# ScalarE takes the norm factor before it rounds weights; first weight loads go out before the conditioning rows; conditioning columns move to other blocks

## The reference

```python
h = rms_norm(x, norm1_g);  proj = h @ w_in            # first layer
x = x + concat([ym, ya]) @ w_out                      # its output product
h2 = rms_norm(x, norm2_g)
x = x + peer(h2, w_query, keys, expert_u, expert_v)   # picked experts
# layers two (neighbourhood attention) and three (sliding window), each:
mod = silu(c) @ w_mod + b_mod                         # six vectors: shift, scale, gate, twice
h = modulate(rmsnorm(x, g_attn), shift, scale);  x = x + gate * (attention(h) @ w_o)
h = modulate(rmsnorm(x, g_ffn), shift2, scale2); x = x + gate2 * ffn(h)

def rms_norm(x, g):
    return x * lax.rsqrt(jnp.mean(x * x, axis=-1, keepdims=True) + EPS) * g
```

## Time and profile before

| | us |
|---|---|
| median of 3 runs | 4173.3 |
| lowest and highest run | 4167.85, 4173.65 |
| the profiled execution, its time | 4169.04 |
| its span | 4167.3 |
| PE busy in it | 3733.9 (90%) |
| DVE busy | 2649.3 (64%) |
| ACT busy | 1393.1 (33%) |
| POOL busy | 1412.3 (34%) |
| mean granted clock of TensorE | 0.938 |

### The profile page before, as it was taken

One profiled execution on the slowest core, in us unless ns is written; L12 is line 12 of the kernel. 1 busy time (PEld: TensorE's weight loads), 2 busy tenths in 40 slices (PEclk: granted clock), 3 DMA queues, 4 the chain that ended last, 5 costly groups with the idle time before them and its releaser, 6 DMA issues. The chain is left out here.

```text
span 4167.3 us, 56565 instructions
## 1 busy us (share of the span) xinstructions
PE 3733.9 (90%) x19126; PEld 3021.2 (72%) x19126; DVE 2649.3 (64%) x5251; ACT 1393.1 (33%) x1937; POOL 1412.3 (34%) x608
## 2 busy tenths in 40 slices
PE   8757789999999989999988989889998977788989
PEld 6634567778888778888877756568887866566867
DVE  7554778888777689999978546574544022744440
ACT  3205223334555322232222137622223122453331
POOL 3002433433333344444443125432222320243433
PEclk9857899999999999999998989989999988899999
DMA  5102344444554666666644340131111110012222
GB/s 208 50 26 89 131 144 139 147 140 143 191 183 159 223 204 189 197 190 197 190 139 155 111 79 1 62 106 66 60 60 49 62 41 33 6 41 91 96 77 89
DMA packets 242904, 475.43 MB, mean 114 GB/s; under 512 B 47307, under 2 KB 127179, under 8 KB 237804
## 3 DMA queue, kind: packets, MB, share of 16 engines
q1 hardware_dynamic: 222300, 433.11, 31.7%
q10 hardware_dynamic: 20480, 40.80, 2.6%
HBM read 397.82 MB, written 71.83 MB: 113 GB/s over the span
## 5 line engine op out<-in xcount | busy, mean ns | idle before, releaser
L329 POOL TENSOR_TENSOR w_low<-w_raw,w_high 128x1024 fp32r<-128x1024 f32 (+1 forms) x204 | 543.6, 2666 | 1079.2 <-ACT w_high L283 1079.2
L227 PE MATMUL psum<-h_high,w_high 128*128 128x512 f32 (+1 forms) x1696 | 627.1, 370 | 113.5 <-DVE h_low L566 78.8
L228 PE MATMUL psum<-h_low,w_high 128*128 128x512 f32 (+1 forms) x1696 | 619.8, 365 | 0.0
L229 PE MATMUL psum<-h_high,w_low 128*128 128x512 f32 (+1 forms) x1696 | 615.1, 363 | 0.0
L283 ACT ACTIVATE w_high<-w_raw 128x1024 fp32r<-128x1024 f32 (+1 forms) x204 | 226.6, 1111 | 905.9 <-PE psum L229 847.4
L1501 POOL TENSOR_TENSOR pick_u_low<-pick_u_raw,pick_u_high 128x1024 fp32r<-128x1024 f32 x128 | 312.3, 2440 | 568.0 <-ACT pick_u_high L1555 568.0
L227 PEld LDWEIGHTS psum<-h_high,w_high 128*128 128x128 f32 x1696 | 323.8, 191 | 191.9 <-issue 102.2
L1755 POOL TENSOR_TENSOR v_low<-v_raw,v_high 128x1024 fp32r<-128x1024 f32 x128 | 307.8, 2406 | 409.8 <-ACT v_high L1742 409.8
L227 PE MATMUL psum<-a_high,v_high 128*128 128x512 f32 x1024 | 399.7, 390 | 13.9 <-DVE v_context L1807 13.9
L227 PE MATMUL psum<-h_high,pick_u_high 128*128 128x512 f32 x1024 | 411.7, 402 | 0.0
L228 PE MATMUL psum<-h_low,pick_u_high 128*128 128x512 f32 x1024 | 403.9, 394 | 0.0
(11 more groups left out here) (378 smaller groups left out, 7090.2 us busy)
## 6 DMA issues: line engine op xcount, KB each, us to landing
pick_u_raw<-in_expert_uT SPq DMA_DIRECT2D x128, 512.0 KB, 3.5
v_raw<-in_expert_v SPq DMA_DIRECT2D x128, 512.0 KB, 3.8
mod_w<-in_w_mod SPq DMA_DIRECT2D x88, 512.0 KB, 3.6
w_raw<-in_ffn_up SPq DMA_DIRECT2D x88, 512.0 KB, 3.4
gelu_dram<-pick_gelu ACTq DMA_DIRECT2D x128, 256.0 KB, 2.0
gates_dram<-gate_plane SPq DMA_DIRECT2D x32, 1024.0 KB, 7.1
g<-gates_dram SPq DMA_DIRECT2D x64, 512.0 KB, 5.1
p<-gelu_dram SPq DMA_DIRECT2D x128, 256.0 KB, 5.0
```

What stands on the lines that cost most here:

```text
L227: nc.tensor.matmul(bank, w_high, x_high, start=first, stop=False)
L228: nc.tensor.matmul(bank, w_high, x_low, start=False, stop=False)
L229: return nc.tensor.matmul(bank, w_low, x_high, start=False, stop=last)
L329: nc.gpsimd.tensor_tensor(w_low[r % 2][:, :, :], raw[r % n_raw][:, :, :], w_high[r % 2][:, :, :].bitcast(F32), ALU.subtract).then_inc(k.w_ ...
```

## The change

Five things are done. (1) `Norm.scalar` is cut in two, and the new `Norm.factor` (Ln and Exp) stands on ScalarE ahead of the rounding of weights 0 and 1. (2) The table load that holds Ln and Exp is issued by ScalarE at the end of the block before, behind its last square; only the first block has it at its own start. (3) In `product`, SP issues the four weight loads of the first pass in a row, and the `mod_w` loads of that pass behind them; in later passes they alternate as before. (4) The columns move: `w_out` has no `side` any more; `w_query` takes columns 16 to 31 in place of 24 to 39; `na_o` takes 32 to 39 with two conditions in place of the second layer's last sixteen with one; `swa_q` takes these sixteen, two to a chunk. (5) In the expert values, `Squares` gets seven square buffers in place of two, GpSimd adds chunks 1 to 4 alone, and TensorE takes the last three squares directly.

```diff
 class Squares:
-    def __init__(self, k, pieces):
+    def __init__(self, k, pieces, at=PICKS_AT, buffers=None, direct=1):
...
     def total(self, pe):
-        pe.wait_ge(self.added.sem, self.added.at(KD - 2))
+        pe.wait_ge(self.added.sem, self.added.at(KD - 1 - self.direct))
         for i, (t0, n) in enumerate(self.pieces):
             self.nc.tensor.matmul(self.k.psum[:, i, 0:n], self.k.const("ones"), self.acc[:, t0:t0 + n], start=True, stop=False)
-        pe.wait_ge(self.squared.sem, self.squared.at(KD))
-        for i, (t0, n) in enumerate(self.pieces):
-            mm = self.nc.tensor.matmul(self.k.psum[:, i, 0:n], self.k.const("ones"), self.slot(KD - 1)[:, t0:t0 + n], start=False, stop=True)
+        for c in range(KD - self.direct, KD):
+            pe.wait_ge(self.squared.sem, self.squared.at(c + 1))
+            for i, (t0, n) in enumerate(self.pieces):
+                mm = self.nc.tensor.matmul(self.k.psum[:, i, 0:n], self.k.const("ones"), self.slot(c)[:, t0:t0 + n], start=False, stop=(c == KD - 1))
...
-        with sp.Fori(0, passes) as it:
+        def load(it, r):
+            sp.wait_ge(k.w_low.sem, k.w_low.at(it * RING + (r + 1)))
+            source = w[it * per + r // parts].rearrange("p (k n) -> p k n", n=P)[:, r % parts * kp:(r % parts + 1) * kp, :]
+            sp.dma_start(raw[r % n_raw][:, :, :], source).then_inc(k.weights_in[r % n_raw].sem, 16)
+
+        for r in range(RING):
+            load(0, r)
+        if side:
             for r in range(RING):
...
+                side.load(sp, 0, r)
+        if passes > 1:
+            with sp.Fori(0, passes - 1) as before:
+                it = before + 1
+                for r in range(RING):
+                    load(it, r)
+                    if side:
+                        side.load(sp, it, r)
...
         if norm:
             norm.squares(act)
+            norm.factor(act)
             round_weights(0, 0)
             round_weights(0, 1)
...
+            nc.scalar.preload_act_table_set("natural_log_exp_and_others")
             return
...
-        product(k, block, t["w_out"], KD, KD, LATENT, high, low, BIG + 2 * KD * SEQ, add_to_x(k, lambda c, i: 1.0, LATENT), full=f.mixT, sums=Squares(k, LATENT),
-                side=Modulation(k, t, ((2 * KD, 1, 2),), 40000, 34816))
+        product(k, block, t["w_out"], KD, KD, LATENT, high, low, BIG + 2 * KD * SEQ, add_to_x(k, lambda c, i: 1.0, LATENT), full=f.mixT, sums=Squares(k, LATENT))
...
-    sums = Squares(k, LATENT)
+    sums = Squares(k, LATENT, at + KD * CTX, KD - 1, 3)
...
-                side=Modulation(k, t, ((3 * KD, 1, 2),), 24832, 26880))
+                side=Modulation(k, t, ((2 * KD, 1, 2),), 24832, 26880))
...
-                side=Modulation(k, t, ((MODS + 4 * KD, 2, 1), (MODS + 4 * KD + 1, 2, 1)), BIG + 2 * KD * TOK, BIG + 2 * KD * TOK + 2 * D, 43008))
+                side=Modulation(k, t, ((4 * KD, 1, 2),), BIG + 2 * KD * TOK, BIG + 2 * KD * TOK + 2 * D, 43008))
...
-                norm=modulated_norm(k, layer, "g_attn", 0, both))
+                norm=modulated_norm(k, layer, "g_attn", 0, both),
+                side=Modulation(k, t, ((MODS + 4 * KD, 2, 1), (MODS + 4 * KD + 1, 2, 1)), BIG + 2 * KD * TOK, BIG + 2 * KD * TOK + 2 * D, 43008))
```

26 lines of the change are left out of this document (12 added, 14 removed).

## The result

| | before | changed |
|---|---|---|
| median, us (6 runs each, same series) | 4172.3 | 4148.3 |
| lowest and highest, us | 4167.85, 4173.65 | 4146.89, 4149.38 |
| time of the profiled execution, us | 4169.04 | 4147.98 |
| its span, us | 4167.3 | 4146.2 |
| mean granted clock | 0.938 | 0.939 |

The account below looks back on a forecast made before the run. The prediction took PE's waits as the bound, chiefly the chain ahead of the first `h_low`. It summed 11.3 + 9.0 - 8.5 - 1.3 + 2.2 = 12.7 us, giving 4160.6 us against the median 4173.3, range 4151 to 4169.

Parts of the forecast that it names:

- The factor first: Six norm blocks: Ln and Exp ahead of both weight roundings let newton and the first matmul start sooner, +11.3 us together.
- the six walks: Norm blocks walked singly: `w_query` 3.5, `na_qk` 6.1, first `ffn_up` 1.4, `swa_q` 1.7, last `ffn_up` 2.4, first block -3.8 us.
- Columns out of `w_out`: `w_out` without columns: 6.8 us from first matmul to `norm_v` and 2.2 us at its start, +9.0 us.
- Columns into `swa_q`: `swa_q` with two columns a chunk: weight loads stand behind row loads waiting for VectorE, -8.5 us, bounds -5 and -12.
- The wait at chunk 4: `swa_q`: weights for chunk 4 come late behind row loads, so that chunk starts 4.9 us late.
- The wait at chunk 7: `swa_q`: chunk 7 is delayed by another 0.9 us.
- the tail of 2 to 3 us: End of `swa_q`: VectorE's last columns end 2 to 3 us after PE.
- SP's new order costs nothing: SP's loads: no change of time, since row loads are needed only after the norm.
- The head norm's table load: Layer three: Silu leaves another table, so the head norm loads one between Ln and Exp, -1.3 us.
- The expert values: End of the expert values: the accumulator is ready sooner and PE does four warm sums, +2.2 us; nothing if cold.
- The splits slip in cheaper: Rival: GpSimd doesn't get between VectorE's back-to-back instructions, up to 2.3 us more in six blocks, near 4147; 8%.
- three slower rivals: `swa_q` dearer and norms less, 4168, 22%; SP's queue serial in `swa_q`, 4190, 4%; weights replace factor wait, 4170.6, 6%.

Follow-up runs that it names:

- factor_only: The kernel before with parts 1 and 2 alone (factor ahead of the roundings, table load in the block before): 4157.3 us, ratio 0.9964 to the kernel before.
- first_block_old_order: The changed kernel with the first block's two roundings ahead of its factor again: 4148.6 us, ratio 0.9947 to the kernel before.
- columns_back: The changed kernel without part 4, the columns back where they were before: 4155.3 us, ratio 0.9962 to the kernel before.
- sums_old: The changed kernel without part 5, GpSimd adding the expert values' squares six times with two buffers: 4151.2 us, ratio 0.9949 to the kernel before.
- vector_splits: The changed kernel with VectorE, not GpSimd, making `w_low` 0 and 1 of the five later norm blocks: 4142.6 us, ratio 0.9932 to the kernel before.
- changed_again: The changed kernel unaltered, run once more in another series: 4149.5 us, ratio 0.9957 to the kernel before.
- columns_only: The kernel before with part 4 alone, columns moved and loads in the old order: 4174.3 us, ratio 1.0004 to the kernel before.
- columns_and_loads: The kernel before with parts 3 and 4, the factor still behind the roundings: 4165.3 us, ratio 0.9991 to the kernel before.

## Why the prediction was right, and where it fell short

The traces gave 21.1 us where the sum had 12.7. Of the 8.4 between them, 4.2 are the norms, 3.1 the columns in `swa_q`, 2.2 the stretch from there to the end of `swa_o`, 0.7 `w_out` and 0.2 the expert values; the start of `w_out` gave 1.9 less than predicted. The terms follow one by one.

**The factor first: right in kind, too small in size.** The blocks did what the walk said: Ln right behind `norm_v`, splits that stop VectorE, `w_query` bound by its weights, a loss in the first block. The step that failed first is the sum of the six walks, 11.3 us, which measured 15.5 in the changed kernel's trace (6.3 less 2.4 for the expert values in `w_query`) and 15.4 in factor_only's. Of the 4.2 between them 0.7 is none of the factor's: the first block's `norm_v` was at 18.13 and is at 17.42, and it lies anywhere between 16.4 and 18.4 in the traces of this case. From `norm_v` to the first matmul that block went from 7.8 to 11.0 us, a loss of 3.2 for the 3.8 predicted. The other 3.5 lie in all six blocks, 0.4 to 0.8 in each. In `na_qk` from `norm_v` to the first matmul it is 2182.54 - 2168.90 = 13.6 us, where the walk had 13.9; in the first block 11.0 where it had 11.5. I had let each split cost VectorE its 2.34 us in full; newton's held instructions lost 2.0 each in the two blocks where they can be read singly (2.58 - 0.56 and 2.45 - 0.43). Two splits in six blocks at 0.3 less are close to the 3.5, but for the other four blocks that cause is argued and not read; in `w_query` the hold was even worse placed than in the walk. One error, made six times with the same sign, was as large as the whole allowance of the range for the norms (some 4), and so nothing was left for the rest.

**Columns out of `w_out`: right.** From first matmul to `norm_v` 454.07 - 405.61 = 48.5 us, as `swa_o` had had 49.15; 7.5 won for 6.8 predicted. The start too: from the first weight load (398.37) to the first matmul 7.24 us, where the earlier trace rows had 9.44, the 2.2 predicted. But the load itself went out late, since TensorE was at half clock at the end of the dilated attention (0.50 from 392 to 398 us, where the kernel before had 1.00 until 396), and the lead grew by only 0.3. From the first block's first matmul to `w_out`'s the traces of this case take from 375 to 380 us (377.4 before, 377.2 in the changed kernel, 380 in factor_only), so that one pair of traces can neither show nor refute this term.

**Columns into `swa_q`: the largest term, -8.5, was mis-sized.** The mechanism was right: chunk 4 was the first to wait, for a weight load behind row loads. Three parts of the term were these. The wait at chunk 4, 4.9 predicted, was 3.2 in the one execution and 4.8 in the other. The wait at chunk 7, 0.9, wasn't there (first_block_old_order has one of 0.60). And the tail of 2 to 3 us, VectorE's columns behind TensorE's end, wasn't there either. VectorE in the changed kernel, the end of `swa_q`:

```profile
3416.68 0.69 DVE L1344 COPY qk<-psum 128x512 f32 x1 [0.25 <-DVE modT L476]
...
3420.51 0.21 DVE L476 TENSOR_SCALAR modT<-mod_sums,params 128x1 f32 x1 [0.26 <-DVE mod_products L468]
...
3421.50 0.69 DVE L1344 COPY qk<-psum 128x512 f32 x1 [0.78 <-PE psum L231]
```

The last two columns are done by 3420.7, and the last copy waits 0.78 us for TensorE, so VectorE had caught up. A chunk without a split beside it takes VectorE 3420.72 - 3416.68 = 4.0 us from copy to last column, under TensorE's 5.6, and there are no splits behind the last rounding. The walk had put one split into every turn of VectorE, 6.5 to 7 us, to the end.

**Part 3, priced at nothing: failed.** "SP's new order costs nothing" looked at its cost and not at what it brings. It is worth 1 to 6 us in the changed kernel, and some 5 with the factor still behind the roundings. Placed are 1.3 us in the norm starts with the factor first (0.5 in `w_query`, 0.7 in `na_qk`, 0.1 in the last `ffn_up`), 4 with the factor behind, where each start waits for weights 1. In `swa_q` the old order leaves weights 3 behind row loads that wait for columns (a wait of 4.99 us at chunk 3), but the columns' cost there, 8.0 and 5.9 us with the old order and 4.1 to 7.4 with the new, doesn't tell the orders apart.

**What I added up as separate terms is not separate.** Columns alone are worth nothing (ratio 1.0004), and in the changed kernel 2 to 7 us. By the runs' values it is the order of loads that decides: with the old order the move is worth about nothing with the factor first or behind, with the new one something. At one place the factor matters as well, since it no longer waits in `swa_q` for weights that the conditioning load delays. The sum had that right by walking `swa_q`'s norm with both edits in place, +1.7 and not -3.4; that the move hangs on part 3 it had not.

**Smaller terms.** The head norm's table load is there as predicted, between Ln and Exp. ScalarE in layer three:

```profile
3506.06 1.28 ACT L1011 ACT_TABLE_LOAD   x1
3507.36 0.84 ACT L1011 ACTIVATE swa_norm_y<-swa_norm_y 32x768 f32<-32x768 f32 x1
```

It is 3507.36 - 3506.06 = 1.30 us from load to Exp, and they are paid. TensorE's wait for the head norm's factor:

```profile
3513.77 0.76 PE L1038 MATMUL psum<-swa_norm_y_high,swa_norm_spread 32*128 32x512 f32 x1 [9.73 <-DVE swa_norm_y_low L1056]
```

It was 8.44 us in the kernel before and is so in the two others without columns in `swa_q`, factor_only and columns_back; in every kernel with them it is 9.72 or 9.73. That is 1.29 us, as the row of the first layer had it. Other differences of that long stretch, 2 us the other way, hide it in the lead. `na_o` came out as said. The expert values did so in the two traces, 2.4 for 2.2, but as sums_old shows, with 0.8 for the fewer adds and 1.6 for a clock that hadn't fallen.

**The rivals.** "The splits slip in cheaper" had the nearest time, 4147, and is false as a mechanism: newton's instructions were held for 2.45 to 2.98 us, and vector_splits, which would have been slower under it, was 6 us faster. The time came near for other reasons. None of the three slower rivals came.

## What to carry to other kernels

Before a part of a change is priced, ask which queue it stands in beside the others: here the move of the columns was, by the runs' values, worth nothing with the loads in the old order, and several us with the weights ahead of the rows, and that order counted most where an engine's next step waited for the second weights of a queue that carried rows as well. Where the same small walk is used in several blocks, its error may have one sign in all of them, so the range must take it times the number of blocks. And work that GpSimd does beside VectorE's critical chain may be cheaper on VectorE itself: 1.22 us in place of a stop of 2.0 us. And one stretch of one trace is one drawing: `swa_q` cost 4.1 to 7.4 us in four executions of the same code, so a difference of 2 us there is no finding.

## What the hardware showed unexpectedly

- A start won just ahead of a slow-clock stretch is sometimes not all kept. With the first matmul of `w_out` at 403.33 and at 405.61, TensorE had been idle for 8 us in both, and came from 0.50 to full clock between 408 and 410 us in both; 2.3 us of lead were 0.8 one chunk later. With the first matmul at 403.96, in changed_again, it came to full clock between 406 and 408, and the lead was kept. What sets the time of the change is not shown by these runs.
- A wait of the same 2.3 us was followed by slow TensorE sums in two kernels (before and factor_only, 2.1 us for the first two matmuls) and by fast ones at granted clock 1.00 in three (columns_only, columns_and_loads and sums_old, 1.1 us), at the end of the expert values.
- Whether VectorE gets in between two of GpSimd's splits hangs on hundredths of a us. In the first `ffn_up` an instruction of newton was already held when the first split ended, and ran ahead of the second (5.54 us for both splits). In `w_query` the first ended near 461.02 + 4.65 / 2 = 463.35, `h_low` 0 came at 463.38, the second split was in, and `h_low` 0 stood for all of it. In columns_back `h_low` 0 came a little ahead of the first split's end and was through in 0.83 us, and the second split held `norm_h` 2:

```profile
471.36 5.11 POOL L342 TENSOR_TENSOR w_low<-w_raw,w_high 128x1024 fp32r<-128x1024 f32 x2 [13.16 <-ACT w_high L294]
...
473.42 0.83 DVE L580 TENSOR_TENSOR h_low<-norm_h,h_high 128x512 fp32r<-128x512 f32 x1 [3.28 <-ACT h_high L533]
```

  There the first matmul comes 10.36 us behind `norm_v`, in the changed kernel 12.29.
- The same program, the same stretch: TensorE's wait at chunk 4 of `swa_q` was 3.18 us in one execution and 4.79 in another, with loads issued at the same distance. It had come through the chunks ahead 1.2 us sooner, with full clock from 14 us behind its first matmul in place of 17.
